# The expert rows of a two-layer transformer kernel: gathered as quarter rows and turned by VectorE instead of by TensorE

## The reference, cut to what matters

```python
MOE_EXPERTS, MOE_TOPK, MOE_FF, MOE_BLOCK = 32, 2, 512, 128

def grouped_expert_mlp(h, expert, weight, w_gu, w_down):
    # every token has two experts; the choices are sorted by expert and put in blocks of 128 rows
    def expert_block(args):
        idx, e = args
        gate, up = jnp.split(h_pad[idx] @ w_gu[e], 2, axis=-1)
        return (jax.nn.silu(gate) * up) @ w_down[e]
    y = lax.map(expert_block, (slot_tok.reshape(n_blocks, MOE_BLOCK), block_e))
    y = y.reshape(-1, d) * slot_w[:, None]
    return jnp.zeros((n + 1, d), y.dtype).at[slot_tok].add(y)[:n]
```

## Time and profile before

| | |
|---|---|
| runs | 2656.98, 2658.21, 2659.9 us |
| profiled execution: span, which is the only time that the page gives of it | 2660.6 us |
| TensorE matmul busy | 2561.7 us, 96% |
| VectorE busy | 1203.4 us, 45% |
| ScalarE busy | 562.7 us, 21% |
| GpSimd busy | 324.8 us, 12% |
| granted TensorE clock, mean | 0.987 |
| DMA bytes | 590.71 MB, mean 222 GB/s |
| largest group | L2702, TensorE, 4608 matmuls of 128x512, 1012.5 us |
| queue of the weights (q1) | 81832 packets, 535.72 MB |
| queue of gathers and scatters (q0) | 15296 packets, 43.31 MB |

### The profile page before, as it was taken

How to read it: one execution, slowest core, us unless ns; L and a number is a source line. 1 busy time by engine, 2 the same in 40 slices (tenths; PEclk the granted TensorE clock), 3 DMA queues, 4 the chain that set the end, 5 groups by cost and what they waited for, 6 DMA issues and landing times.

```text
span 2660.6 us, 34138 instructions
## 1 busy us (share of the span) xinstructions
PE 2561.7 (96%) x13314; PEld 1294.0 (49%) x13314; DVE 1203.4 (45%) x2576; ACT 562.7 (21%) x1181; POOL 324.8 (12%) x395
## 2 busy tenths in 40 slices
PE   6999999999999899999999899999999999999997
PEld 3444456547655444433333344577745444444333
DVE  3264357238777632222222475677787611111114
ACT  3211111028632100000000221488721000000002
POOL 0043200212011100000000012000011000000002
PEclk9999999999999999999999999899999999999998
DMA  9710111123123799999998810300024799999997
GB/s 381 306 17 0 67 48 61 35 37 88 59 104 126 292 398 420 414 378 373 411 394 334 347 51 0 71 2 2 1 76 160 271 390 423 417 423 417 407 417 263
DMA packets 99885, 590.71 MB, mean 222 GB/s; under 512 B 21727, under 2 KB 25015, under 8 KB 74761
## 3 DMA queue, kind: packets, MB, share of 16 engines
q1 hardware_dynamic: 81832, 535.72, 51.4%
q0 software_dynamic: 15296, 43.31, 4.1%
q10 hardware_dynamic: 2592, 9.44, 0.9%
HBM read 554.98 MB, written 45.99 MB: 226 GB/s over the span
## 4 chain that ended last, share of the span: by engine, by line
PE 84%; DMA 7%; DVE 6%; SPq 1%; issue 1%; POOL 0%; ACT 0%; POOLq 0%; DVEq 0%; ACTq 0%
PE PS L2702 34%; PE PS L1054 11%; PE PS L1250 5%; PE PS L1906 5%; PE PS L2139 4%; PE PS L1918 4%; PE PS L1929 4%; PE PS L1440 4%; PE PS L1723 4%; DMA ar<-in_expert_w_gu_dram 3%; DMA ar<-in_ada_w_dram 1%; PE PS L2707 1%; DMA ar<-yd 1%; DMA h2d<-ar 1%; PE PS L2712 1%
## 5 line engine op out<-in xcount | busy, mean ns | idle before, releaser
L2702 PE MATMUL PS<-ar 128*32 128x512 f32 (+2 forms) x4608 | 1012.5, 595 | 20.3 <-DMA ar<-in_expert_w_gu_dram 14.8
L2702 PEld LDWEIGHTS PS<-ar 128*32 128x32 f32 (+2 forms) x4608 | 372.2, 137 | 624.2 <-issue 616.9
L1054 PE MATMUL PS<-ar 128*128 128x512 f32 (+1 forms) x768 | 314.0, 565 | 4.2 <-DMA ar<-in_swa_w_in_dram 2.3
L2847 ACT ACTIVATE ar<-PS 128x512 f32<-128x512 f32 x48 | 28.7, 597 | 1068.3 <-PE PS L2702 1068.3
L1054 PEld LDWEIGHTS PS<-ar 128*128 128x128 f32 x768 | 144.2, 191 | 150.3 <-issue 141.5
L1962 DVE CUSTOM_DVE_ANT_0 ar<-PS,ar 128x640 f32<-128x640 f32 (+2 forms) x208 | 158.0, 797 | 71.5 <-PE PS L1906 71.3
L2139 PE MATMUL PS<-ar 128*128 128x512 f32 x392 | 175.2, 597 | 1.5 <-ACT ar L2270 0.9
L2919 DVE TENSOR_TENSOR ar<-PS,ar 128x512 f32<-128x512 f32 x48 | 33.2, 692 | 315.2 <-ACT ar L2847 315.2
L2942 DVE TENSOR_TENSOR ar<-PS,ar 128x1024 f32<-128x1024 f32 x48 | 58.8, 1225 | 242.2 <-PE PS L2702 137.1
L2925 DVE COPY ar<-PS 128x512 f32<-128x512 f32 x48 | 33.2, 692 | 279.7 <-PE PS L2712 279.7
L2017 ACT ACTIVATE ar<-ar 128x641 f32<-128x641 f32 (+4 forms) x208 | 159.5, 772 | 0.8 <-DVE ar L1962 0.8
(11 more groups left out here) (342 smaller groups left out, 2506.1 us busy)
## 6 DMA issues: line engine op xcount, KB each, us to landing
ar<-in_expert_w_gu_dram SPq DMA_DIRECT2D x128, 2048.0 KB, 16.1
ar<-in_expert_w_down_dram SPq DMA_DIRECT2D x64, 2048.0 KB, 15.5
ar<-in_ada_w_dram SPq DMA_DIRECT2D x24, 2048.0 KB, 14.7
ar<-yd SPq DMA_DIRECT2D x36, 512.0 KB, 5.4
ar<-in_ab_w_in_dram SPq DMA_DIRECT2D x6, 2048.0 KB, 9.3
h2d<-ar ACTq DMA_DIRECT2D x18, 512.0 KB, 2.9
ar<-in_x_dram SPq DMA_DIRECT2D x8, 512.0 KB, 13.5
ar<-in_ab_w_out_dram SPq DMA_DIRECT2D x1, 4096.0 KB, 27.0
```

Of the source, the lines that this page charges most:

```text
L1054: mm = nc.tensor.matmul(out_, lhs, rhs, start=(k == 0), stop=(k == KC - 1))
L2702: mm = nc.tensor.matmul(out[at:to], lhsT[:, at:to], w[:, k, cols], start=start, stop=stop)
```

## The change

Blocks 0 and 1 of each stage are as before. From block 2 on, the DRAM tensor `h2d` is read as 4 x 1280 quarter rows of 1 KB. Four indirect DMAs (j = 0 to 3) fill the four column quarters of `hb[b % 2]`: partition 32a + i, column quarter j takes quarter a of token 32j + i. One VectorE transpose, which turns each 32x32 block within its 32 partitions, then writes the same `hbT` as before, from SBUF to SBUF; it takes the place of the eight TensorE transposes and of the copy out of PSUM. The indices of the quarters (`src4_i`, four for each block and partition) are made by a multiplication of `src_i` with a mask on VectorE (in `route_slots`), four matmuls with a 128x32 matrix that fold 128 partitions onto 32, one for each group of output partitions (`route_fold`, after `up(0)`), and one VectorE instruction, 4 x index + quarter (`route_quarters`, after `mul(0)`). GpSimd waits for that before block 2's gather. `gather_quarters(b)` waits for the VectorE transpose of block b-2. The counts of the semaphores of the gathers follow: 16 for blocks 0 and 1, 64 for each other block. Three constants of 32, 4 and 1 columns are added to `cst`. The code for overflow blocks (experts with more rows than their slots hold) stays as it was.

```diff
--- before.py
+++ after.py
@@ program @@
+        srcq = R(51456, 4 * EXP)
+        src4_i = R(51584, 4 * EXP).bitcast(I32)
+        h2q = h2d.rearrange("t (a n) -> (t a) n", a=4)
...
+        def hb_in(b):
+
+            return 16 + 64 * (b // 2)
...
@@ route_slots @@
-            slot_places(dve, ch, Vb, src_i[:, 0:nb], dst_i[:, 0:nb], key[:, 0:nb], nb, 0).then_inc(S(f"{n}_idx"), 1)
+            ch(slot_places(dve, ch, Vb, src_i[:, 0:nb], dst_i[:, 0:nb], key[:, 0:nb], nb, 0))
+            V.tensor_tensor(srcq[:, 0:4 * nb].rearrange("p (b j) -> p b j", j=4), bcast_in(src_i[:, 0:nb], 4),
+                            bcast_mid(cst[:, C_QUAD:C_QUAD + 4], nb), ALU.mult).then_inc(S(f"{n}_idx"), 1)
...
+        def route_fold(pe, l):
+            pe.wait_ge(*done(f"r{l}_idx", 1))
+            for a in range(4):
+                mm = nc.tensor.matmul(PS[32 * a:32 * a + 32, 7, 128:128 + 4 * n_blk[l]], cst[:, C_FOLD:C_FOLD + 32], srcq[:, 0:4 * n_blk[l]],
+                                      start=True, stop=True)
+            mm.then_inc(S(f"r{l}_shift"), 1)
+
+        def route_quarters(dve, l):
+            dve.wait_ge(*done(f"r{l}_shift", 2))
+            nc.vector.tensor_scalar(src4_i[:, 0:4 * n_blk[l]], PS[:, 7, 128:128 + 4 * n_blk[l]], 4.0, cst[:, C_PART:C_PART + 1], ALU.mult, ALU.add)\
+                .then_inc(S(f"r{l}_idx"), 1)
@@ moe_pe @@
-                pe.wait_ge(*done(f"{n}_hb{b % 2}", 16 * (b // 2 + 1)))
+                pe.wait_ge(*done(f"{n}_hb{b % 2}", hb_in(b)))
...
-                if b + 1 < nb:
-                    turn(b + 1)
+                if b == 0:
+                    turn(1)
                 up(b)
+                if b == 0:
+                    route_fold(pe, l)
@@ moe_dve @@
             def rows_in(b):
+                if b >= 2:
+                    dve.wait_ge(*done(f"{n}_hb{b % 2}", hb_in(b)))
+                    dve.wait_ge(*done(f"{n}_gu", b - 1))
+                    V.transpose(hbT[b % 2].rearrange("p k (j m) -> p k j m", j=4), hb[b % 2].rearrange("p (j m k) -> p k j m", j=4, k=KC))\
+                        .then_inc(S(f"{n}_hbT"), 1)
+                    return
                 dve.wait_ge(*done(f"{n}_tr", b + 1))
-                if b >= 2:
-                    dve.wait_ge(*done(f"{n}_gu", b - 1))
...
             mul(0)
+            route_quarters(dve, l)
@@ moe_pool @@
+            def gather_quarters(b):
+                pool.wait_ge(*done(f"{n}_hbT", b - 1))
+                c = moe.blocks[b]["col"]
+                for j in range(4):
+                    pool.indirect_dma_start(out=hb[b % 2][:, 256 * j:256 * j + 256], out_offset=None, in_=h2q,
+                                            in_offset=bass.IndirectOffsetOnAxis(ap=src4_i[:, 4 * c + j:4 * c + j + 1], axis=0),
+                                            bounds_check=4 * TOK - 1, oob_is_err=False)\
+                        .then_inc(S(f"{n}_hb{b % 2}"), 16)
...
-            pool.wait_ge(*done(f"r{l}_idx", 1))
+            pool.wait_ge(*done(f"r{l}_idx", 2))
             for b in range(2, nb):
-                gather(b)
+                gather_quarters(b)
                 if b >= 4:
                     scatter(b - 4)
```

More of the change, by code:

```diff
@@ L61 @@
 C_KEY = C_SL + P
-C_N = C_KEY + 32
+C_FOLD = C_KEY + 32
+C_QUAD = C_FOLD + 32
+C_PART = C_QUAD + 4
+C_N = C_PART + 1
 def rank_bounds(l):
@@ L132, in tables @@
     c[:, C_KEY:C_KEY + 32] = np.arange(32) - np.where(np.arange(32) < 2, 1e6 * (2 - np.arange(32)), 0)
+    c[:, C_FOLD:C_FOLD + 32] = p[:, None] % 32 == np.arange(32)[None, :]
+    c[:, C_QUAD:C_QUAD + 4] = p[:, None] // 32 == np.arange(4)[None, :]
+    c[:, C_PART] = p // 32
     inv = (np.float32(10000.0) ** (-np.arange(16, dtype=np.float32) / np.float32(16))).astype(np.float32)
@@ L333, in program @@
         share(("{}_h2o",), "o0", "o1", 16 * NT)
-        share(("{}_cnt", "{}_first", "{}_ord", "{}_perm", "{}_shift", "{}_idx", "{}_ctl"), "r0", "r1", 1)
+        share(("{}_cnt", "{}_first", "{}_ord", "{}_perm", "{}_ctl"), "r0", "r1", 1)
         share(("{}_wx",), "r0", "r1", 2)
@@ L387, in program @@
         n_blk = [len(moe_blocks(l)) for l in range(2)]
+        def hb_in(b):
+            return 16 + 64 * (b // 2)
         kept = {Moe(1).pieces[i]["buf"] for part in "gud" for i, _, _ in Moe(1).at[part, n_blk[1] - 1]}
         yg[1] += [[R(piece_at[q] + 2048 * h + 1024 * j, D) for j in range(2)] for q in range(6) if q not in kept for h in range(2)]
-        share(("{}_tr", "{}_hbT", "{}_ga", "{}_gu", "{}_silu", "{}_mul", "{}_gt", "{}_guT", "{}_dn", "{}_y"), "m0", "m1", n_blk[0])
+        share(("{}_tr",), "m0", "m1", 2)
+        share(("{}_shift", "{}_idx"), "r0", "r1", 2)
+        share(("{}_hbT", "{}_ga", "{}_gu", "{}_silu", "{}_mul", "{}_gt", "{}_guT", "{}_dn", "{}_y"), "m0", "m1", n_blk[0])
         for q in range(6):
@@ L393, in program @@
         for q in range(2):
-            share((f"{{}}_hb{q}", f"{{}}_yo{q}"), "m0", "m1", 16 * len(range(q, n_blk[0], 2)))
+            share((f"{{}}_yo{q}",), "m0", "m1", 16 * len(range(q, n_blk[0], 2)))
+            share((f"{{}}_hb{q}",), "m0", "m1", hb_in(n_blk[0] - 1 - (n_blk[0] - 1 - q) % 2))
         share(("{}_x",), "c0", "c1", NT)
@@ L419, in program @@
         for q, after in enumerate(("fx_in", "fx_out")):
-            share(("{}",), f"m1_hb{q}", after, 16 * len(range(q, n_blk[1], 2)))
+            share(("{}",), f"m1_hb{q}", after, hb_in(n_blk[1] - 1 - (n_blk[1] - 1 - q) % 2))
         for before, after in (("ss1", "fin_ss"), ("n1_ms1", "fin_ms"), ("n1_rt1", "fin_rt")):
@@ L2998, in gather @@
             def gather(b):
-                if b >= 2:
-                    pool.wait_ge(*done(f"{n}_tr", b - 1))
                 c = moe.blocks[b]["col"]
-                pool.indirect_dma_start(out=hb[b % 2], out_offset=None, in_=h2d,
-                                        in_offset=bass.IndirectOffsetOnAxis(ap=(first_i if b < 2 else src_i)[:, c:c + 1], axis=0),
+                pool.indirect_dma_start(out=hb[b], out_offset=None, in_=h2d,
+                                        in_offset=bass.IndirectOffsetOnAxis(ap=first_i[:, c:c + 1], axis=0),
                                         bounds_check=TOK - 1, oob_is_err=False)\
-                    .then_inc(S(f"{n}_hb{b % 2}"), 16)
+                    .then_inc(S(f"{n}_hb{b}"), 16)
+            def gather_quarters(b):
[6 more added lines that the diff above has]
+                        .then_inc(S(f"{n}_hb{b % 2}"), 16)
             def scatter(b):
```

## The result

The changed kernel takes 2637.06 us (median of four runs, 2634.41 to 2645.28), the one before 2658.82 us (2656.98 to 2659.90): ratio 0.9927, 95% interval 0.991 to 0.9944. The medians differ by 21.8 us; by the ratio it is 19.4 us. Forecast were 11.9 us and 2646.3 us, with a range down to 2641.0; the result lies outside it, on the fast side. On another chip, with five rounds, the same program gave 2639.53 us and 0.9938 [0.9925, 0.9951], 16.5 us. The mean of the two ratios, 0.9933, is 17.8 us.

What follows compares the result with a forecast made beforehand. TensorE bounds the first stage after about 1122 us, the weight queue its start and the second stage. 12.6 + 1 + 2.5 - 3.2 + 0 - 1 = 11.9 us faster: 2646.3 us from 2658.2, range 2641 to 2664.

Steps and rivals of the forecast that it cites:

- (a): Both expert stages: TensorE transposes go, 39.6 us; won: 12.6 us late first stage, 1 us before, 2.5 us second stage.
- The end of each stage moves with it.: After each stage: the tail, such as ada weight loads after the first, keeps its length and only shifts.
- First stage, before that: First stage up to 1122 us: weight queue full, so saved TensorE time becomes waits; gain 1 us, of 0 to 8.1.
- (b): Gathers from the third block on: four quarter-row transfers cost more packet time where DMA is the bound; 3.2 us lost.
- rival B: Gathers: every quarter row takes its own queue turn, so blocks start 5.3 us late; 2659 us; chance 14%.
- (c): GpSimd issues four gathers a block, the last quarter 4 us later, landing after 15 us; hidden, the scatter behind it too.
- (d): VectorE transpose replaces the 1.22 us copy out of PSUM: 1.28 us, bounds 0.6 to 2.6, hidden at either end.
- (e): Routing tail at the first stage's start: 0 us, with 5 us of slack; 5 to 8 us if landing takes twice as long.
- (f): TensorE clock: more and longer waits for weights bring more half clock; 1 us lost, of 0 to 8.
- A: Both stages: weights have no slack, gathers use none; only 6.1 us faster, 2652 us; chance 19% together with D.
- D: TensorE: four more waits, each followed by 1.2 GHz, 2 us each; 2654 us; chance 19% together with A.
- C: Gathers: 1 KB packets cost 97 ns, so the queue is the bound throughout; 39 us slower, 2697 us; chance 10%.

Runs made afterwards that it cites:

- experiment 7: Tiny GpSimd writes added in the second stage: 24 in the kernel before, 2657.16 us; 24 in the changed kernel, 2639.27 us; 120 in the changed kernel, 2638.84 us.
- experiment 4: Kernel before and changed kernel, each loading only half of every up piece in the second stage: 2644.71 us (0.9948) and 2605.52 us (0.9804).
- experiment 3: Kernel before with quarter rows, still turned by TensorE: 2657.81 us, 1.0002; changed kernel with whole rows turned by VectorE, second stage 0.9943, first stage 551.4 us long.

## Why the prediction was wrong

The direction and, for the stages, the place were right, the size was not: 11.9 us forecast, 21.8 and 16.5 measured. By the means over traces of the same form:

| | without | with | won | forecast, net |
|---|---|---|---|---|
| first stage | 564.7 (4 traces) | 550.4 (7) | 14.3 | 12.1 |
| second stage | 529.3 (5) | 529.5 (6) | -0.2 | -0.2 |
| end, from the last scatter | 48.3 (5) | 44.2 (8) | 4.1 | 0 |

They add up to 18.2 us, against 17.8 in the mean of the timed ratios. The forecast column is the sum's terms split over the stages, the clock's 1 us in halves: 12.6 + 1 less 1.0 for packets and 0.5 for the clock; 2.5 less 2.2 and 0.5. The 25.1 us between the two profiled executions are more, because that of before was a long one, with 566.8 and 532.1 us in its stages against means of 564.7 and 529.3. The 21.8 us between the medians of the main result are 3.6 above the sum as well; the interval of its ratio, 15 to 24 us, holds both, and the rest isn't assigned.

(a) Blocks after the crowded stretch: 12.6 us forecast. From the matmul at 1121.5 us in before, and the same one in every other trace, to the end of the stage, it is 358.1 us in all six traces with TensorE's turn in this order, alike to 0.01 us, and 345.6 to 346.9 in the seven changed ones: 12.1 us won on average, 12.5 in the two main traces. Right, and a block takes 21.49 us.

**The largest step that failed is in the sum: "The end of each stage moves with it."** The end of the kernel did not only move, it became 4.1 us shorter. No reading of the profile of before led there. Some 1.6 us of it are half clock behind waits for loads of the results; why those waits became shorter isn't found (experiment 7).

**The other is (a), "First stage, before that":** "I put this part at a gain of 1 us, out of 0 to 9 x 0.90 = 8.1 us, because the nearest row says full." With its packets and the clock that was a net loss of 0.5 us. The part up to 1121.5 us takes 205.0 to 208.7 us in the four traces with TensorE's turn (mean 206.6) and 203.1 to 205.6 in the seven changed ones (mean 204.4): a gain of 2.2 us, in the two main traces 4.3. The same code varies by up to 3.7 us there, so the size of this gain is loose. A share of 0.99 was read as full, although the row beside it showed the same engines at 425 GB/s and this one at 408: 4% of 130 us would be 5 us of room. Before's form also runs there at 415 and 416 GB/s in other traces, so the 408 belonged in part to this one execution. And only 2.6 us of waiting stood in the first stage. A queue that makes TensorE wait so little is nearly balanced with it, and not the bound throughout; that is argued from the waits, no run tests it.

Second stage: 2.5 us forecast before the costs, -0.2 after them, -0.2 measured. The net is right in part by luck, since neither the 2.5 us nor the costs taken off it show by themselves. The reading of the bound was right (experiment 4): the waits grew to 22.8 us (30 was said), the share stayed at 1.00 and the length within 3 us.

(b) 3.2 us for quarters: experiment 3 has 0.5 us, -1.9 to 2.9, over the whole kernel, and in the two stages whole rows differ from quarters by +1.0 and -0.2 us under the VectorE turn. (The term counts 8 blocks of the first stage where (a) counts 9, which is 0.2 us.) So 3.2 is too high for the whole, if barely by the interval; if the short end in that run's trace is a gift of the quarters, their price in the stages under TensorE's turn may be near it. The packets came out to the one: 17408 - 15296 = 2112 = 44 x 48. Quarters share packets, and rival B is refuted: a transfer lands after 8.0 us in the middle and 12.1 at the most, not after 20.

(c) Hidden, as forecast. The scatter of a block is issued at 1155.73 us, behind four quarters issued from 1143.17 on.

(d) 1.28 us forecast, 2.03 measured, inside the bounds of 0.6 to 2.6 and hidden as was said for either end.

(e) 0 us: the start of the first stage moved by 0.6 us, and no late gather after the routing but the one wait of 5.6 us on VectorE, which no one on the chain waited for.

(f) 1 us lost by the half clock: there are more such spells in the second stage (13.7 us, 3.4 before), where the weights are the bound and its length shows no loss; in the first none that could be priced. One spell that the kernel before had at its end, worth 1.6 us, the changed one has not.

Rivals A and D fall with C: all three put the time above 2650.

## What to carry to other kernels

A share of 0.99 alone doesn't say that a queue is the bound. Look at GB/s beside it and at how long the fast engine really waits, and before pricing a few per cent, at a second execution: the same stretch of the same code ran at 408 to 416 GB/s. When a change moves a stage, move the window with it; the fixed window 2289 to 2591 us showed a share of 0.97 where the stage was as full as before. Work taken off an engine is won where that engine is the bound and nowhere else, which loading a sixth less of the weights showed in one pair of runs. And the two kinds of stretch repeat differently: where TensorE was the bound, 358 us came out alike to 0.01 us in six traces, and in the part before it, where TensorE also waited for weights, 207 us varied by 3.7. One profile of each kernel is enough for a term of the first kind, not for one of 1 to 3 us of the second. Time the runs beside the traces: a pair of traces said 19.8 us for a stage where the medians showed nothing new.

## What the runs showed of the hardware

- The VectorE turn of 128x1024 f32 in 32x32 blocks takes 2.03 us, 1.7 times a copy of the same shape out of PSUM (1.22 us).
- Four indirect gathers of 128 rows of 1 KB in place of one of 128 rows of 4 KB add no packets but those of completion (2112 for 132 more transfers, 16 each). Each lands 8.0 us after its issue (median), against 10.9 for the whole rows; but the fourth is issued 4 us after the first, and a block's rows are complete 12.8 us after the first issue (median of the 21 blocks whose landings the trace of the changed kernel has).
- GpSimd's instructions come 8 KB at a time, 128 recorded instructions apart (560, 688, 816, 944 in these traces). At the first output transfer the engine stood for 4.9 to 6.0 us where such a load fell on it. 24 added instructions took such a hold away, 120 brought one about.
- After waits of TensorE of 2 to 5 us its granted clock is 0.50 (1.2 GHz) in many cases, and not in all: with the same code the spell came in one trace of the first stage and stayed out of three others, and after 3.7 us of waiting for the last load it came in one kernel and stayed out in another. Six of the last products take 4.48 us at 0.50 and 2.85 at full clock.
